# 256-column products in the stages on b_buf and c_buf, and a_buf with the low part behind the high part in one row

## What is computed

```
qkv = rms(x) @ w_qkv;  h = x + attention(q,k,v) @ w_o            # 2048 -> 3*2048, 2048 -> 2048
h = h + square(relu(rms(h) @ w1)) @ w2                           # 2048 -> 8192 -> 2048
h = concat(16 meta tokens, rms(h))                               # second block
u, gb, gc, v, ga, gbr = split(rms(h) @ w_in)                     # 2048 -> 6*2048
y_a = (multiscale_pool(u) @ pool_w) * pool_scale
y_b = (gb * causal_conv(gc * v)) @ conv_out_w
h = h + (sigmoid(ga)*y_a + sigmoid(gbr)*y_b) @ w_o2
h = h + (silu(rms(h) @ w_gate) * (rms(h) @ w_up)) @ w_down       # 2048 -> 5632 -> 2048
out = rms(h)[16:]
```

## Time and profile before

| | us |
|---|---|
| runs, median (lowest to highest) | 2584.97 (2584.65 to 2585.15) |
| the profiled execution | 2584.9 |
| its span | 2583.2 |
| PE busy in the span | 2572.6 |
| granted TensorE clock, mean | 0.999 |
| DMA, mean | 188 GB/s |

### The profile page before, as it was taken

The page is one execution under the profiler, slowest core; times in us unless marked ns, Lnnn a source line. Parts: engine busy times, 40 slices in busy tenths (PEclk is TensorE's granted clock), DMA queues, the critical chain, the costliest instruction groups (busy, mean ns, idle before and its releaser), DMA issues.

```text
span 2583.2 us, 40378 instructions
## 1 busy us (share of the span) xinstructions
PE 2572.6 (100%) x16053; PEld 2315.2 (90%) x16053; DVE 1622.4 (63%) x1398; ACT 1190.6 (46%) x1181; POOL 141.3 (5%) x87
## 2 busy tenths in 40 slices
PE   9999999999999999999999999999999999999998
PEld 9999999888888888899899988888888888888887
DVE  6577766656656556886654776566756545654555
ACT  5455554444444444544533344444544434443444
POOL 0000100000000000000200530000000000000001
PEclk9999999999999999999999999999999999999999
DMA  7554456556555555555555555555555555555563
GB/s 262 182 168 159 163 181 192 188 191 194 196 187 189 193 195 193 181 180 187 188 182 188 184 181 194 185 190 195 195 185 190 182 193 195 191 191 192 191 211 131
DMA packets 243954, 485.26 MB, mean 188 GB/s; under 512 B 7728, under 2 KB 8944, under 8 KB 243696
## 3 DMA queue, kind: packets, MB, share of 16 engines
q1 hardware_dynamic: 243520, 483.12, 55.9%
q10 hardware_dynamic: 320, 0.53, 0.1%
HBM read 481.53 MB, written 2.10 MB: 187 GB/s over the span
## 4 chain that ended last, share of the span: by engine, by line
PE 98%; DVE 1%; DMA 0%; ACT 0%; issue 0%; POOL 0%; SPq 0%; DVEq 0%; ACTq 0%; POOLq 0%
PE ps L1330 42%; PE ps L1340 21%; PE ps L1387 14%; PE ps L1368 8%; PE ps L1395 7%; PE ps L1374 4%; PE ps L1443 0%; PE ps L1497 0%; PE ps L1409 0%; DMA raw<-in_sb_w_qkv_dram 0%; PE ps L1431 0%; PE ps L1502 0%; PE ps L1480 0%; PE ps L1434 0%; DVE wlo L775 0%
## 5 line engine op out<-in xcount | busy, mean ns | idle before, releaser
L775 DVE TENSOR_TENSOR wlo<-raw,whi 128x1024 fp32r<-128x1024 f32 x900 | 1115.9, 1265 | 908.7 <-ACT whi L568 901.2
L568 ACT ACTIVATE whi<-raw 128x1024 fp32r<-128x1024 f32 x900 | 935.7, 1058 | 1304.0 <-PE ps L1340 843.0
L1330 PE MATMUL ps<-b_buf,whi 128*128 128x512 f32 x2688 | 643.1, 392 | 0.0
L1330 PEld LDWEIGHTS ps<-b_buf,whi 128*128 128x128 f32 x2688 | 492.7, 188 | 96.8
L1340 PEld LDWEIGHTS ps<-b_buf,wlo 128*128 128x128 f32 x2688 | 331.4, 188 | 14.3
L1340 PE MATMUL ps<-b_buf,wlo 128*128 128x256 f32 x2688 | 333.9, 277 | 0.0
L1387 PE MATMUL ps<-a_buf,whi 128*128 128x258 f32 (+4 forms) x2560 | 330.9, 282 | 0.5 <-ACT a_buf L585 0.5
L1387 PEld LDWEIGHTS ps<-a_buf,whi 128*128 128x128 f32 x2560 | 315.7, 188 | 1.0 <-ACT a_buf L585 0.7
L1330 PE MATMUL ps<-c_buf,whi 128*128 128x512 f32 x1280 | 306.3, 392 | 0.0
L1330 PEld LDWEIGHTS ps<-c_buf,whi 128*128 128x128 f32 x1280 | 234.6, 188 | 46.0
L1330 PE MATMUL ps<-a_buf,whi 128*128 128x512 f32 x768 | 185.7, 394 | 0.0
(11 more groups left out here) (202 smaller groups left out, 1472.0 us busy)
## 6 DMA issues: line engine op xcount, KB each, us to landing
raw<-in_mlp_w_dram SPq DMA_DIRECT2D x128, 1024.0 KB, 5.1
raw<-in_w_in_dram SPq DMA_DIRECT2D x96, 1024.0 KB, 4.9
raw<-in_w_gate_up_dram SPq DMA_DIRECT2D x88, 1024.0 KB, 4.9
raw<-in_sb_w_qkv_dram SPq DMA_DIRECT2D x44, 1024.0 KB, 5.0
raw<-in_w_down_dram SPq DMA_DIRECT2D x44, 1024.0 KB, 5.1
raw<-in_sb_w_o_dram SPq DMA_DIRECT2D x16, 1024.0 KB, 5.1
raw<-in_conv_out_w_dram SPq DMA_DIRECT2D x16, 1024.0 KB, 5.1
raw<-in_w_o_dram SPq DMA_DIRECT2D x16, 1024.0 KB, 5.1
```

Of the source, the lines that this page charges most:

```text
L568: act.activation(whi[:, unit_of(n, u)], raw[:, n % RAW, u * UK:(u + 1) * UK, :], ACT.Copy).then_inc(w_hi, 1)
L775: dve.tensor_tensor(wlo[:, s], raw[:, n % RAW, u * UK:(u + 1) * UK, :], cast(whi[:, s]), ALU.subtract).then_inc(w_lo, 1)
L1330: high = pe.matmul(ps[:, 4 * half + j, :].rearrange("p (a n) -> p a n", a=2), whi[:, unit_of(n - back, u), kt, j * P:(j + 1) * P], buf[:, ...
```

## The change

The table of pairs is gone: `PAIRED` becomes `FOUR` (kinds whose panel uses four banks), and each `Panel` has `pairs`. `pairs=RUNS` keeps the old form: ga, gb, gbr and the first two panels of co. A number means that only so many joint products are made, at the panel's very start, and that all else in it is 256 columns wide, each column tile with a bank of its own and everything summed in the bank's first half. That number is 4 in panel 0 of w1_0, 5 in panel 1; 5 in the first up panel of gu_0; 4 in the first gate panel of gu_1 and of gu_2. It is 0 in the other 55 panels. So 60 of the 62 panels change.

In panels with `pairs=0`, `cross_out` and its add fall away; the counts in `KINDS` follow. co becomes one unrolled stage, gu_1 and gu_2 get a first iteration of their own.

a_buf becomes `[P, NT, ROW]` with ROW = 576: a row is 16 meta tokens, 256 high, 256 low, and the 16 low meta tokens in reverse order, 2,304 bytes apart. A joint product on a_buf now reads 512 columns in one piece. In u, gc and vv the product with X_lo starts at the tokens and runs on into the reversed meta tokens; its meta part lands behind column 272 and DVE brings it home with a small copy and add at each panel's end. `ms` moves to another place.

```diff
+ROW = 2 * TW + 32
...
-PAIRED = ("add", "relu2", "res2", "resb", "ga", "gb", "gbr", "co", "gate", "up")
+TWO_PARTS = dict(act=1, mid=1)
+FOUR = ("add", "relu2", "res2", "resb", "ga", "gb", "gbr", "co", "gate", "up")
...
-            add("w1_0", 1, [Panel("relu2", "w1", 0, lambda i, g=g: g * PW, src="C", needs="w_o") for g in range(4)],
+            add("w1_0", 1, [Panel("relu2", "w1", 0, lambda i, g=g: g * PW, src="C", needs="w_o", pairs=(4, 5, 0, 0)[g])
+                            for g in range(4)],
...
+        ready[f"gu_{f}"] = (gate_up(f"gu_{f}_first", done, 1, norm=None if f else 2, pairs=(4, 0) if f else (0, 5)) +
+                            gate_up(f"gu_{f}_rest", done + 1, n - 1, j0=1))
...
-        a_buf, a_off = place("a_buf", [P, 2, NT, TW], F32R)
+        a_buf, a_off = place("a_buf", [P, NT, ROW], F32R)
...
+        a_hi, a_lo, b_hi, b_lo = a_buf[:, :, 0:TW], a_buf[:, :, T:2 * TW], b_buf[:, 0], b_buf[:, 1]
+        m_lo = a_buf[:, :, TW + T:2 * TW][:, :, ::-1]
+        a_pair = a_buf[:, :, M:M + 2 * T].rearrange("p t (a n) -> p a t n", a=2)
...
+                if kind in WIDE:
+                    spare = M - WIDE[kind]
+                    step(dve.tensor_copy(S2[:, :, 0:spare], ps[:, 4 * half:4 * half + 4, TW:TW + spare][:, :, ::-1]))
+                    early = ps[:, 4 * half:4 * half + 4, WIDE[kind]:M]
+                    step(dve.tensor_tensor(early, early, S2[:, :, 0:spare], ALU.add))
+                if two:
                     step(dve.tensor_tensor(full[:], n, full[:], ALU.add))
+                    n = full[:]
...
+                        products = [(kt, x, j) for kt, x in kts for j in range(JT)]
+                        joint = products[:p.pairs] if first else []
+                        for kt, x, j in joint:
+                            pe.matmul(ps[:, 4 * half + j, :].rearrange("p (a n) -> p a n", a=2),
+                                      whi[:, s, kt, j * P:(j + 1) * P], buf[:, :, x, tok], start=kt == 0, stop=False,
+                                      skip_group_check=True)
+                        for part, dst, cols in ((x_hi_, outs, tok), (x_lo_, lows, low_tok)):
...
+                            for kt, x, j in products[len(joint):]:
+                                pe.matmul(dst[j], whi[:, s, kt, j * P:(j + 1) * P], part[:, x, cols],
+                                          start=first and kt == 0 and part is x_hi_ and (alone or j % 2 == 0),
+                                          stop=False, skip_group_check=True)
```

More of the change, by code:

```diff
@@ L97, with __init__, counts @@
 class Panel:
-    def __init__(self, kind, weight, row0, col, chunks=CH, tile0=0, src=None, needs=None):
+    def __init__(self, kind, weight, row0, col, chunks=CH, tile0=0, src=None, needs=None, pairs=0):
         self.kind, self.weight, self.row0, self.col = kind, weight, row0, col
         self.chunks, self.tile0, self.src, self.needs = chunks, tile0, src, needs
+        self.pairs = pairs
+    def counts(self):
+        more = TWO_PARTS if self.pairs else {}
+        return {k: KINDS[self.kind].get(k, 0) + more.get(k, 0) for k in NAMES}
+ATTN = Panel("attn", None, 0, None)
 class Stage:
@@ L149, in enter @@
             self.per["chunk"] += p.chunks
-            for k, v in KINDS[p.kind].items():
+            for k, v in p.counts().items():
                 self.per[k] += v
@@ L160, in event, with closed @@
         for k, v in KINDS[kind].items():
+            self.n[k] += v
+    def closed(self, panel):
+        for k, v in panel.counts().items():
             self.n[k] += v
@@ L212, in make_stages, with loop2 @@
         ("u0", "u1", "u2", "u3"), norm=1)
[L214 to L218, removed]
+    def loop2(name, kind, weight, col0, src, needs=None, pairs=0, **kw):
+        add(name, 2, [Panel(kind, weight, 0, lambda i, h=h: col0 + i * 2 * PW + h * PW, src=src, needs=needs,
+                            pairs=pairs) for h in range(2)], (kind,), **kw)
+    loop2("ga", "ga", "w_in", 4 * D, "A", pairs=RUNS)
     add("pw", 1, [Panel("pw", "pool_w", g * PW, lambda i: 0, chunks=1, tile0=g * JT, src="B", needs="u")
@@ L639, in evac @@
                     return
-                if not KINDS[kind].get("act") or kind == "add":
+                if not KINDS[kind].get("act"):
                     return
@@ L936, in norm, with evac @@
                 dve.wait_ge(rstd_ready, k + 2)
-            def evac(kind, half, j):
+            def evac(p, half, j):
+                kind, two = p.kind, int(bool(p.pairs))
                 mid[0] = 0
@@ L1195, in mask, with evac @@
                 last.then_inc(after, 1)
-            def evac(kind, j):
+            def evac(p, j):
+                kind, two = p.kind, int(bool(p.pairs))
                 if kind == "ga":
@@ L1306, in token_rows @@
                 last.then_inc(rr_mm, 1)
-            bufs = {"A": (a_buf, M), "B": (b_buf, 0), "C": (c_buf, 0), "D": (d_buf, 0)}
+            bufs = {"A": (a_pair, 0), "B": (b_buf, 0), "C": (c_buf, 0), "D": (d_buf, 0)}
             def three(out, w_h, w_l, x_h, x_l, start, stop):
@@ L1379, in chunk @@
                         tok = slice(lo_col, TW) if wide_ else slice(off, off + T)
[L1380 to L1389 removed]
+                        x_hi_, x_lo_, low_tok = (a_hi, a_lo, slice(M, TW + M - lo_col)) if wide_ else (hi, lo, tok)
@@ new lines, in chunk @@
+                        alone = wide_ or p.kind in FOUR
+                        if wide_:
+                            outs = [ps[:, 4 * half + j, lo_col:TW] for j in range(JT)]
+                        elif alone:
+                            outs = [ps[:, 4 * half + j, 0:T] for j in range(JT)]
+                        else:
+                            outs = [ps[:, 4 * half + j // 2, (j % 2) * T:(j % 2 + 1) * T] for j in range(JT)]
+                        lows = [ps[:, 4 * half + j, M:TW + M - lo_col] for j in range(JT)] if wide_ else outs
```

152 lines of the change are left out of this document (70 added, 82 removed).

## The result

| | before | after |
|---|---|---|
| runs, median (lowest to highest), us | 2584.91 (2584.61 to 2585.15) | 2596.16 (2595.82 to 2596.85) |
| span of the profiled execution, us | 2583.2 | 2594.2 |
| products on PE | 16053 | 19871 |

The changed kernel is slower by 0.4%: ratio 1.0044, 95% interval 1.0033 to 1.0055. The forecast was 2567.5.

What follows compares the result with a forecast made beforehand. PE, busy 2572.6 of 2583.2 us, bounds the kernel and only its pace changes; -11.0 - 4.5 - 1.4 + 0.3 - 0.7 = -17.3 us on 2584.9 makes 2567.6, stated as 2567.5; range 2550 to 2600.

Steps and rivals of the forecast that it cites:

- entry remainder: From w_o into w1_0: PE's count of three is 2, so four joint products bring 0 and the 113.33 ns pace.
- first rival: Behind norms, 48 products shift the count of three, five joint products miss: +32.5 us, 2600; chance 20%, both or the first.
- The quick pace does not hold over whole chunks: b_buf and c_buf stages: all 256-column products fall to 117.8 ns, +39.9 instead of -11.0 us, 2618.5; chance 8%.
- partly lost: Operand changes within a unit or loop borders keep a tile at 343.0 ns: 2578.5, or no change; chance 12%.
- b_buf and c_buf panels: 60 panels, 3840 tiles, go from 343.0 to 340.0 ns a tile with 256-column products at 113.33: -11.0 us.
- q and k: 1536 products go from 117.6 ns to w_o's 117.9: +0.3 us; other end -6.6.
- ga, gb, gbr: 768 still paired tiles on a_buf save 5.9 ns each as rows lie alike within 256 bytes: -4.5 us.
- u, gc, vv: 2304 products of 258 to 272 columns, kept at the slower pace, save 0.6 ns each by aligned rows: -1.4 us.
- v: 384 products with weights loaded from a_buf get half of a 3.7 ns saving each: -0.7 us, ends 0 and -1.4.
- ACT and DVE: 60 copies and 60 adds go, two small operations come in 12 wide panels; nobody waits for them: 0.
- the rule weighed in the prediction: About 2.5 ns fixed per product: 3818 more products would add an estimated 9.5 us and the change would lose.

Runs made afterwards that it cites:

- pad128: The changed kernel with 128 unused bytes behind rr1, where ms stood: 2568.04 us, ratio 0.9935 to the kernel before.
- door3: The changed kernel with 3 instead of 4 joint products at the head of w1_0's first panel: 2569.82 us, ratio 0.9942 to the kernel before.
- row2240: door3 with a_buf's rows 2,240 bytes apart, no multiple of 256: 2576.63 us, ratio 0.9969 to the kernel before.
- a_only: The kernel before with only the new a_buf rows and ms at its new place, panels paired as before: 2581.71 us, ratio 0.9988.
- pairs_only: The kernel before with only the new pairing and ms at its new place, a_buf's rows old: 2599.91 us, ratio 1.0059.
- shift0: door3 with a_buf and all behind it 192 bytes further, token rows 0 instead of 64 bytes from the weights' rows within 256: 2653.09 us.

## Why the prediction was wrong, step by step

**The step that failed** is the entry remainder: "At the entry from w_o the remainder e must have e + 15 not 0 and e + 1 + 15 + 15 = 0: e = 2". For the kernel before that was right, and I carried it over to the changed kernel as if it were a property of w_o. It depends on where buffers that are used before the door lie, and the diff's smallest line, `ms` at another place, changed it to 0. I had read that line and given it no cost. Price: 724.01 - 697.00 = 27.0 us; without it the changed kernel takes 2568.04 (pad128), 0.5 us from the forecast. The mechanism of the large terms was right; that it comes to within 0.5 us is luck, for three small terms below missed by 1 to 2 us each and largely cancelled in the sum.

**The rivals.** The measured 2596 lies near the first rival's 2600, but its mechanism, that the 48 products behind a norm move the remainder, is not what happened: in door3, pad128 and at gu_0 they stand there and the five joint ones hit. What I left out is a miss at the first door, and that it takes the second with it, since the norm keeps what it finds and adds one. "The quick pace does not hold over whole chunks" is refuted: in pad128 PE goes from behind w1_0's second door to u, 672.43 us, at 113.33 ns a product, none above 115:

```profile
425.00:1097.43 672.43, 672.43 (x5936) 672.43 (x5934) 394.17 (x329) 286.95 (x275) 0.00 (x0) 1.00 0.59 193
```

That refutes "partly lost" as well: a stage of 768 products takes 87.04 us, 113.33 each.

**The terms,** on pad128, where the doors hit:

- b_buf and c_buf panels: 702.90 to 697.00 (-5.9), -2.8 in co to gu_0, -2.7 in gu_1 and gu_2: -11.4, forecast -11.0.
- q and k: forecast +0.3. All before w1_0 goes from 400.55 to 400.43 us in spite of v's +1.1 below, so the rest, w_o with it, gives -1.2: k's and w_o's stretches behind the attention's products are quick in pad128 (114.5 for 118.9 ns over 48 products, three times, and 113.9 for 118.3 over 96). The forecast had both stages drag throughout.
- ga, gb, gbr: -4.6, forecast -4.5; row2240 shows that the reason was the right one. In a_only it comes alone.
- u, gc, vv: forecast -1.4, measured -0.9 + 0.6 = -0.3. The size was off: a_only has the +0.6 and pairs_only not, so aligned rows make these products 0.4 ns longer, while u's -0.9 comes with the pairing.
- v: forecast -0.7; its first 48 products went from 11.06 us to 11.19, 230.4 to 233.3 ns, about +1.1 for 384. I had put the surplus down to unlike rows; shift0 takes 10.90 us (227.2 ns) for them. Here it is the distance 0 that is quick, which a_buf's old rows had in one row of four and the new ones never; that this is why the old rows were quicker is not shown.
- ACT and DVE: 0, as forecast. The one wait that grew, at pw's second panel (0.5 to 0.9 us), lengthens that stage by 0.04 us (23.36 to 23.40).

The split of a product costs nothing fixed that the traces show: 256 columns take 113.33 ns and 512 in dn_1, with the roles changed, 226.7, twice that, and w1_0 to w2_3 takes 697.00 us with 3 products a tile against 702.90 with 2. This bears on the rule weighed in the prediction (the Trainium skill, TensorE: Matmul & The Clock Gate, "Wait — 56ns, not 53.3ns?"), by which pad128 would have lost; it is 16.8 us faster than before on the same chip.

The Trainium skill (SBUF — State Buffer, "SBUF: two separate sides") says that PE's port never waits for anyone, and its next section gives weight loading a read port of its own. DVE and ACT do the same work in door3's w1_1 and in shift0's (50.72 and 50.73 us, 36.83 and 36.71), yet a product takes 113.3 or 120.0 ns by where the tokens' rows lie. Whether that is a wait at a port is not shown; what the trace decides is that a product's time depends on its operands' addresses.

## What to carry to other kernels

Where PE is busy for the whole span, put the rows of its two operands on a common step (here a multiple of 256 bytes) and try how far one lies from the other within it: between the best and the worst place this kernel's time differs by 3.5%, with the same instructions. A state that the engine carries along is no constant of a stage: before relying on it, pin everything that feeds it, the addresses of unrelated small buffers included, or read it anew from the first trace of the changed kernel. And a diff's line that only moves a buffer needs a term of its own in the sum.

## What the runs showed of the hardware

- The pace of 256-column products depends on where the tokens' rows lie within 256 bytes, told here as the distance from the weights' rows: 113.3 or 117.8 ns at 64 and 192, 117.3 or 118.7 at 160, 118.7 at 128, 120.0 at 0 and 96 (in w1_1 and wo2; at 64 the dragging one from the changed kernel).
- With the roles changed (activations loaded, 512 weight columns streamed), the distance 0 is the quickest of those tried instead: 227.2 ns in v against 233.3 at 64.
- At 64 a few joint products choose between the two paces, and PE keeps the quick one for 672 us without another (pad128).
- 128 unused bytes ahead of the small buffers and the attention's decide 28.1 us of 2596 (after and pad128), 27.0 of them between w1_0 and w2_3.
